# The column sums of the conditioning vector as two products of rounded parts, with two moving columns

## The reference

```python
c_act = jax.nn.silu(c)                      # 1 x 1024
for l in range(DEPTH):                      # 2 layers
    mod = (c_act @ w_ada[l] + b_ada[l]).reshape(B, N_SUB, 3, D_MODEL)   # 9216 values
    x = x + 0.5 * gate(0) * _swiglu(norm_mod(x, 0), w_ffn_up[l, 0], w_ffn_down[l, 0])
    x = x + gate(1) * _mixer(norm_mod(x, 1), ...)
    x = x + 0.5 * gate(2) * _swiglu(norm_mod(x, 2), w_ffn_up[l, 1], w_ffn_down[l, 1])
```

## Time and profile before

| | |
|---|---|
| median of 3 runs | 3784.11 us (3781.92 to 3784.44) |
| the profiled execution | 3782.52 us, of it the span of the trace 3780.8 us |
| instructions in the trace | 52186 |
| mean granted TensorE clock | 0.984 |
| DMA | 359.84 MB, 95 GB/s in the mean |

### The profile page before, as it was taken

How to read it: one execution, slowest core, us unless ns; L and a number is a source line. 1 busy time by engine, 2 the same in 40 slices (tenths; PEclk the granted TensorE clock), 3 DMA queues, 4 the chain that set the end, 5 groups by cost and what they waited for, 6 DMA issues and landing times.

```text
span 3780.8 us, 52186 instructions
## 1 busy us (share of the span) xinstructions
PE 3608.8 (95%) x19222; PEld 2906.2 (77%) x19222; DVE 2171.2 (57%) x3513; ACT 1203.7 (32%) x1787; POOL 362.2 (10%) x545
## 2 busy tenths in 40 slices
PE   8989899999989899989999998999999999999999
PEld 6768688877768688878887766888778877667887
DVE  5867588645877678545544655555343336554332
ACT  3344333323334333222222344222222223442221
POOL 1101011100201011101110101111000001010000
PEclk9999999999999999999999999999999999999999
DMA  4300255532300255425543302455333332113333
GB/s 111 83 23 3 60 158 159 143 91 74 82 13 17 72 160 162 134 84 156 161 143 104 80 24 61 138 162 146 106 89 100 87 103 70 34 45 89 96 88 95
DMA packets 580059, 359.84 MB, mean 95 GB/s; under 512 B 20414, under 2 KB 559792, under 8 KB 579888
## 3 DMA queue, kind: packets, MB, share of 16 engines
q1 hardware_dynamic: 554480, 281.43, 27.0%
q0 software_dynamic: 25408, 76.11, 6.7%
HBM read 355.35 MB, written 2.10 MB: 95 GB/s over the span
## 4 chain that ended last, share of the span: by engine, by line
PE 80%; DVE 11%; issue 3%; DMA 2%; ACT 2%; DVEq 1%; POOL 0%; ACTq 0%; SPq 0%; POOLq 0%
PE ps L1431 17%; PE ps L1433 16%; PE ps L1432 16%; PE ps L1680 6%; PE ps L1684 6%; PE ps L1683 6%; DMA wada<-in_w_ada 2%; DVE wl L2253 1%; PE ps L1596 1%; PE ps L1576 1%; PE ps L1865 1%; PE ps L1554 1%; DVEq L2256 1%; PE ps L1529 1%; PE ps L1643 1%
## 5 line engine op out<-in xcount | busy, mean ns | idle before, releaser
L1431 PE MATMUL ps<-hh,wh 128*128 128x512 f32 x3168 | 1261.1, 398 | 54.2 <-DVE wl L2253 22.8
L1433 PE MATMUL ps<-hh,wl 128*128 128x512 f32 x3168 | 1242.8, 392 | 0.0
L1432 PE MATMUL ps<-hl,wh 128*128 128x512 f32 x2912 | 1142.3, 392 | 0.0
L2253 DVE TENSOR_TENSOR wl<-wring,wh 128x1024 fp32r<-128x1024 f32 x500 | 611.4, 1223 | 779.6 <-ACT wh L841 771.8
L841 ACT ACTIVATE wh<-wring 128x1024 fp32r<-128x1024 f32 x528 | 556.6, 1056 | 1032.3 <-PE ps L1433 524.6
L1431 PEld LDWEIGHTS ps<-hh,wh 128*128 128x128 f32 x3168 | 600.2, 189 | 209.0 <-issue 49.7
L1433 PEld LDWEIGHTS ps<-hh,wl 128*128 128x128 f32 x3168 | 599.8, 189 | 128.0
L1432 PEld LDWEIGHTS ps<-hl,wh 128*128 128x128 f32 x2912 | 552.7, 190 | 112.6 <-issue 1.9
L1680 PE MATMUL ps<-ah,wh 128*128 128x512 f32 x1056 | 411.9, 390 | 2.0 <-DVE wl L2253 2.0
L1684 PE MATMUL ps<-ah,wl 128*128 128x512 f32 x1056 | 410.9, 389 | 0.0
L1683 PE MATMUL ps<-al,wh 128*128 128x512 f32 x1056 | 410.9, 389 | 0.0
(11 more groups left out here) (421 smaller groups left out, 3390.3 us busy)
## 6 DMA issues: line engine op xcount, KB each, us to landing
wring<-in_w_ffn_up SPq DMA_DIRECT2D x176, 512.0 KB, 4.9
wada<-in_w_ada POOLq DMA_DIRECT2D x384, 192.0 KB, 2.7
wring<-in_w_in SPq DMA_DIRECT2D x98, 512.0 KB, 5.1
wring<-in_ffn_w_up SPq DMA_DIRECT2D x88, 512.0 KB, 4.9
wring<-in_w_ffn_down SPq DMA_DIRECT2D x64, 512.0 KB, 3.9
wring<-in_w_out SPq DMA_DIRECT2D x32, 512.0 KB, 5.0
wring<-in_ffn_w_down SPq DMA_DIRECT2D x32, 512.0 KB, 3.9
wring<-in_w_ffn_down SPq DMA_DIRECT2D x16, 384.0 KB, 3.5
```

Of the source, the lines that this page charges most:

```text
L1431: pe.matmul(dst, w, h, start=first, stop=False)
L1432: pe.matmul(dst, w, hlo, start=False, stop=False)
L1433: return pe.matmul(dst, wlo, h, start=False, stop=last)
L2253: v.tensor_tensor(wl[:, w, :, :], wring[:, p, h, :, :], wh[:, w, :, :].bitcast(F32), ALU.subtract)\
```

## The change

`ada_out` is no longer read by TensorE. When the eighth step of a group is done, VectorE waits for it, copies it to `ada_hi` (type float32r, that is rounded), waits for that copy, and writes the difference to `ada_lo`. A semaphore of its own, `ada_parts`, tells PE, which waits for it in the place of `ada_step`. PE multiplies each of the three pieces twice, the high part and then the low part, into the same place in PSUM, and with two moving columns of rounded ones (`ones_r`, made by GpSimd at the start) instead of one. So each piece gives two equal columns, and the copy at step 18 takes every second one. The two unused functions `norm` and `root` go, and `std` and `rstd` shrink from 512 to 128 columns.

```diff
+        ones_r = sb("ones_r", P, 2, dt=F32R)
...
+        ada_hi = sb("ada_hi", P, ADA_W, dt=F32R)
+        ada_lo = sb("ada_lo", P, ADA_W, dt=F32R)
...
+            g.tensor_copy(ones_r[:, :], ones[:, 0:2]).then_inc(pool_order.sem, 1)
+            pool_order.next(g)
...
             def conditioned(n):
 
-                ada_step.next(pe, KD)
+                ada_parts.next(pe)
                 for j in range(AJ):
-                    m = pe.matmul(ps[:, 5, bass.ds(n * AJ + j, 1)], ada_out[:, j * P:(j + 1) * P], ones[:, 0:1],
-                                  start=True, stop=True)
+                    col = ps[:, 5, bass.ds(n * (2 * AJ) + 2 * j, 2)]
+                    pe.matmul(col, ada_hi[:, j * P:(j + 1) * P], ones_r[:, 0:2], start=True, stop=False)
+                    m = pe.matmul(col, ada_lo[:, j * P:(j + 1) * P], ones_r[:, 0:2], start=False, stop=True)
                 m.then_inc(ada_used.sem, 1)
...
                 i.then_inc(ada_step.sem, 1)
+                if k == KD - 1:
+                    done = ada_step.seen[id(v)]
+                    v.wait_ge(ada_step.sem, done[0] + done[1])
+                    link(v.tensor_copy(ada_hi[:, :], ada_out[:, :]))
+                    v.tensor_tensor(ada_lo[:, :], ada_out[:, :], ada_hi[:, :].bitcast(F32), ALU.subtract)\
+                        .then_inc(ada_parts.sem, 1)
...
-                        v.tensor_copy(dst, ps[:, 5, 0:AJ * NA])
+                        v.tensor_copy(dst, ps[:, 5, 0:2 * AJ * NA:2])
```

More of the change, by code:

```diff
@@ L177, in program @@
         sq = sb("sq", P, 4, T)
-        std = sb("std", P, T)
-        rstd = sb("rstd", P, T)
+        std = sb("std", P, P)
+        rstd = sb("rstd", P, P)
         ident = sb("ident", P, P)
@@ L384, in program @@
         ada_used = ev("ada_used")
+        ada_parts = ev("ada_parts")
         small_lo = ev("small_lo")
@@ L880, in square @@
                 n_sq[0] += 1
[L882 to L896, removed]
             def sum_square(k, src):
@@ L1662, in ffn @@
                 if ada:
-                    per[ada_step] = KD
+                    per[ada_parts] = 1
                 with loop(pe, NF // 2 - 1, per) as i:
@@ L2265, in filled @@
                 return (n_mm[0] - 1) % 4
[L2267 to L2272, removed]
             def row_roots(n):
@@ L2476, in ffn @@
                 if ada:
+                    per[dve_order] += 1
                     per.update({ada_loaded[0]: 4 * 16, ada_loaded[1]: 4 * 16, ada_step: KD, ada_used: 1})
```

## The result

The changed kernel takes 3830.89 us (median of 4 runs, 3825.74 to 3832.91) where the kernel before takes 3783.02 (4 runs beside it). The ratio is 1.0122, with a 95% interval of 1.0110 to 1.0134: by the medians 48 us slower, by the interval 42 to 51. The forecast was 3799, its range ended at 3808. The direction was right and the size was wrong by a factor of three, and the experiments show that most of the time comes from a place that the prediction cost at nothing.

The account below looks back on a forecast made before the run. VectorE was taken to bound the first block's up stages, PE the second's and the down projections. 3782.5 us plus 16 for VectorE plus 0 for PE gave 3798.5, stated as 3799, range 3787 to 3808.

Parts of the forecast that it names:

- What bounds each stage: Up stages: VectorE sets the pace in the first block's two, PE in the second block's, at 22.45 us a group.
- PE: six loads for six, 0: PE's group products: six rounded matmuls are bound by six loads, as the three float32 ones were, so 0 us.
- Rival one: PE's group products: rounded loads are cheaper, saving 0.34 or 0.47 us in 28 groups, so 3790 or 3786; chance 0.14.
- The changed addresses I cost at 0: Buffers whose addresses the edit shifts: claimed to cost 0 us.
- The forecast for the second block: Second block's up stages: added vector work is hidden and the groups' period stays 22.45 us.
- VectorE's work, 16 us: First block's two up stages: copy and subtraction add 1.27 us a group, net 0.85, making 8 us a stage.
- What is given back, 0.42: First block's loops: added work covers the next group's second-step DMA wait, giving back 0.42 us a group, bounds 0 to 0.75.
- Rival two: First block: the vector work is hidden there too, the conditioning's DMA chain being the real pace; 3783 to 3784, chance 0.06.
- three: Faster: vector work hidden and cheaper loads in all 48 groups, 3768, or 3778 with half hidden; chance 0.05.
- Rival four: First block's loops: nothing is given back and gaps are longer, 1.4 us in 20 groups, 28 us, so 3810; chance 0.09.

Follow-up runs that it names:

- e10: Kernel before with four wada buffers instead of two for the conditioning weights, std and rstd shortened, arena in place: 3776.70 us, 0.9985.
- e9: Kernel before plus only VectorE's rounding copy and subtraction, results unread by PE, hh and arena in place: 3789.78 us, 1.0019.
- e5: Changed kernel with ones_r put into unused bytes behind epsc, so the arena stands where it was before: 3790.03 us, 1.0022 against the kernel before.
- e1: Kernel before with one unused tile of 32 bytes per partition ahead of the arena: 3830.38 us, 1.0127.
- e14: Changed kernel with 224 unused bytes ahead of the arena, 256 with the 32 of ones_r: 3791.66 us, 1.0032 against the kernel before.
- e6: Kernel before with only the rounded weight tiles wh and wl moved up 32 bytes inside the arena: 3855.16 us, 1.0195.
- e4: Kernel before with 64 unused bytes ahead of the arena: 3839.75 us, 1.0148.
- e7: Kernel before with 128 unused bytes ahead of the arena: 3799.85 us, 1.0043.
- e15: Kernel before with 192 unused bytes ahead of the arena: 3823.84 us, 1.0114.

## Why the prediction was wrong

- *What bounds each stage* was read rightly. VectorE set the pace in the first block (e10 takes waits from VectorE and the time falls, e9 adds work and it grows), PE in the second.
- *PE: six loads for six, 0.* Right. The group's passes stand 0.11 us apart, and the period in the second block of e5 is 22.45 as before. Rival one, cheaper rounded loads, falls: they have 191 ns also where only two columns stream beside them. (Its price was misread besides: 56 ns is what such a load would need for its columns, not what it would save. The saving is 105 - 56 = 49 ns, 0.29 a group.) The Trainium skill's fast weight load (TensorE: Matmul & The Clock Gate, section Weight-path perf modes) isn't seen with this type: a rounded load takes the 191 ns of a float32 one. Nor does the Trainium skill's rule of four passes for true float32 (FP8 and Floating Point Precision, section TensorE Precision Notes) show as a gain: three float32 products and six rounded ones both stand in the trace as six passes 0.11 us apart. How many passes stand behind one such record no run shows.
- *The changed addresses I cost at 0.* This is the step that failed: a term put at nothing without a reason. It measures about 40 of the 48 us, and 48 where VectorE's work is not there. e1 shows it without any instruction of the change, e5 and e14 show the change without it, e6 shows that the distance from the streamed tile to the weights is enough for it. The forecast for the second block, a period of 22.45, failed by this alone: it is 23.08.
- *VectorE's work, 16 us.* The mechanism was right, the size was twice the 8.3 measured in e5. The copy has 0.36 us and the subtraction 0.56, as worked out. Mis-sized were the gaps: 0.17 and 0.12 were taken from L2436 and L2437 in the loop, and the new ones measure 630.58 - 629.92 - 0.62 = 0.04 and 630.97 - 630.58 - 0.36 = 0.03. It is not the instructions that differ. Ahead of the loop the same two lines of the kernel before have gaps of 0.03 and 0.04 as well:

```profile
486.24 0.68 DVE L2443 TENSOR_TENSOR sq<-sq 128x512 f32<-128x512 f32 x1
486.95 0.43 DVE L2436 CAST ah<-sq 128x512 fp32r<-128x512 f32 x1
487.42 0.69 DVE L2437 TENSOR_TENSOR al<-sq,ah 128x512 fp32r<-128x512 f32 x1
```

In the loop each of the two has a register instruction ahead of it that, in the trace, begins only 0.04 us after the vector instruction before has ended (at 634.70 and 635.29 beside the earlier trace rows). The new ones have a single one each, which runs beside the vector instruction before. So the added work is 0.04 + 0.36 + 0.03 + 0.56 + 0.06 = 1.05 us in this turn and not 1.27. In the second feed-forward it is 0.83, since what follows starts 0.06 behind `ada_lo` there and had started 0.22 behind the eighth step.
- *What is given back, 0.42.* Of the two waits that the prediction names, 0.67 is that of a sixth step, in the middle of a group, where the added work covers nothing; only the 0.23 belongs to a second step. The waits at the second step went, the others stayed, 4.0 of 8.3 us. From the eighth step to the second step of the next group VectorE took 4.53 us in the turn of the earlier trace rows and takes 5.28 in e5; over the second to the ninth group the trace has 0.62 more in the first feed-forward and 0.40 in the second, and not 0.85. And PE enters each stage with some lead (the first period of either stage is 22.45 with e5 as before), so the first groups cost less: 4.3 and 2.6 us a stage came of it, not 8.
- *In the changed kernel as it stands that term is hardly to be seen.* PE's own period with the slow passes is 23.06 (e1), about what VectorE needs with the added work (23.1 to 23.2 in e5). From the first group to the eleventh the two stages take 231.7 + 230.8 us with the change and 230.3 twice in e1, 1.9 us more. The change at 3830.9 and e1 at 3830.4 don't differ by their runs. Between 580 and 700 us one wait of PE's weight loads is left:

```profile
PEld ps L1421 <- issue: 0.7, 1, 0.7
```

- *Rivals.* None named the placement. Rival two (the work is hidden) falls with the 8.3 us of e5 and the 7.0 of e9, three with it. Rival four (nothing given back) was the slowest and would still have ended at 3810.

## What to carry to other kernels

A tile that is added, shrunk or left out moves all that lies behind it. Before costing such an edit at nothing, work out the distance from the streamed operand to the weight tile of the heavy matmuls, before and after; where it was a multiple of 256 bytes keep it one, if need be with a few unused bytes. As the share of the distance between two streamed tiles is open, keep that one too. If a trace shows many untouched matmuls a few ns longer with equal counts and an equal clock, add an equal pad to the kernel before: one run tells. And take the price of a wait between two dependent instructions from a pair with the same register work ahead of the wait, and give back only those waits that lie behind the added work.

## What the runs showed of the hardware

- The passes of 512 rounded columns follow each other after 0.2267 us where the weights lie a multiple of 256 bytes from what is streamed, and after 0.233 at 32 bytes beyond. That is 3% of each such pass for a shift of 32 bytes, and 1.3% of this kernel's time (e1).
- The loss is not monotonic in the distance: 48, 57, 18 and 44 us at 32, 64, 128 and 192 bytes (e1, e4, e7, e15).
- A load of 128 rounded weights takes 191 ns, as one of float32 weights does; six passes with two moving columns stand 0.11 us apart, as six with one do.
- A dependent VectorE instruction starts 0.03 to 0.04 us behind the one it waits for, where no register instruction begins in between (e5, and ahead of the loop in the kernel before), and 0.12 to 0.17 where one does.
